# Pooling mixer of a two-layer diffusion step: padded input written by the producer, edge columns scaled apart, residual updates between the window groups

## The reference

```python
def pool_mixer(h, w, scale):
    for j, win in enumerate((2, 4, 8, 16)):
        xg = hf[..., j * 256:(j + 1) * 256]
        lo = jnp.clip(t - win // 2, 0, s)
        hi = jnp.clip(t + win // 2, 0, s)
        mean = (cs[:, hi] - cs[:, lo]) / (hi - lo)      # cs: running sum over tokens
        outs.append((mean - xg) @ w[j])
    return jnp.concatenate(outs, axis=-1) * scale
...
x = x + g1 * pool_mixer(modulate(x, norm_mix_g, sh1, sc1), ...)
h = modulate(x, norm_ffn_g, sh2, sc2)
x = x + g2 * peer(h, ...)
```

## Time and profile before

| | us |
|---|---|
| median of 3 runs | 3579.02 (3578.78 to 3579.57) |
| the profiled execution | 3577.18 |
| its span, first to last instruction | 3575.4 |
| TensorE busy | 3155.2 (88%) |
| VectorE busy | 3021.8 (85%) |
| ScalarE busy | 1053.4 (29%) |
| GpSimd busy | 1889.5 (53%) |

### The profile page before, as it was taken

How to read it: one execution, slowest core, us unless ns; L and a number is a source line. 1 busy time by engine, 2 the same in 40 slices (tenths; PEclk the granted TensorE clock), 3 DMA queues, 4 the chain that set the end, 5 groups by cost and what they waited for, 6 DMA issues and landing times.

```text
span 3575.4 us, 49897 instructions
## 1 busy us (share of the span) xinstructions
PE 3155.2 (88%) x15686; PEld 2598.6 (73%) x15686; DVE 3021.8 (85%) x5339; ACT 1053.4 (29%) x1587; POOL 1889.5 (53%) x1412
## 2 busy tenths in 40 slices
PE   6988999378999999999998496088999999999997
PEld 3554555167899999999997254077899999999996
DVE  1645279887999999999998679896999999999998
ACT  2122111043333333333333210044333333333332
POOL 0000012276677887777774012276677777767663
PEclk8999999689999999999999798589999999999999
DMA  4122144036999999999997010036999999999995
GB/s 195 47 94 74 71 174 166 14 159 255 408 409 406 399 403 387 401 404 405 400 396 299 25 48 0 0 164 270 407 410 408 403 404 393 409 409 400 404 405 214
DMA packets 244633, 995.72 MB, mean 278 GB/s; under 512 B 22608, under 2 KB 72528, under 8 KB 204880
## 3 DMA queue, kind: packets, MB, share of 16 engines
q0 software_dynamic: 147456, 536.94, 37.9%
q1 hardware_dynamic: 97104, 457.81, 32.5%
HBM read 941.44 MB, written 53.22 MB: 278 GB/s over the span
## 4 chain that ended last, share of the span: by engine, by line
PE 58%; DVE 23%; issue 9%; DMA 6%; POOL 2%; ACT 1%; DVEq 0%; POOLq 0%; SPq 0%; ACTq 0%
PE bankA L1094 7%; PE bankA L1092 7%; PE bankA L1093 7%; PE bankD L1080 6%; PE bankD L1105 5%; PE bankD L1106 5%; PE bankD L1104 5%; PE bankA L1177 3%; DMA rows<-in_v,idxc 3%; DVE acc L953 3%; PE bankA L1106 2%; PE bankA L1105 2%; PE bankA L1104 2%; PE bankD L1223 2%; DMA rows<-in_u,idxc 1%
## 5 line engine op out<-in xcount | busy, mean ns | idle before, releaser
L492 POOL DMA_INDIRECT rows<-in_u,idxc x512 | 748.6, 1462 | 233.7 <-issue 133.0
L492 POOL DMA_INDIRECT rows<-in_v,idxc x512 | 679.0, 1326 | 256.3 <-issue 134.3
L1092 PE MATMUL bankA<-hh,uh 128*128 128x384 f32 x2048 | 690.5, 337 | 22.7 <-ACT htok L562 13.8
L1094 PE MATMUL bankA<-hh,ul 128*128 128x384 f32 x2048 | 690.1, 337 | 0.0
L1093 PE MATMUL bankA<-hl,uh 128*128 128x384 f32 x2048 | 688.5, 336 | 0.0
L953 DVE SCALAR_TENSOR_TENSOR acc<-rows,a,acc 128x1024 f32<-128x1024 f32 x512 | 635.4, 1280 | 13.8 <-DMA rows<-in_v,idxc 12.5
L944 DVE CUSTOM_DVE_ANT_0 rows<-rows,htok 128x1024 f32<-128x1024 f32 x512 | 607.3, 1220 | 21.0 <-DMA rows<-in_u,idxc 19.2
L454 POOL TENSOR_TENSOR mask<-mask,topf 128x1280 f32<-128x1280 f32 x32 | 91.8, 2890 | 969.2 <-DVE mask L874 969.2
L546 ACT ACTIVATE wt<-bankA 128x384 f32<-128x384 f32 x256 | 125.9, 492 | 995.6 <-PE bankA L1094 756.4
L1177 PE MATMUL bankA<-hT,wch 128*128 128x512 f32 (+1 forms) x1344 | 385.7, 447 | 35.5 <-ACT hT L607 21.8
L1092 PEld LDWEIGHTS bankA<-hh,uh 128*128 128x128 f32 x2048 | 386.8, 189 | 35.1 <-ACT htok L562 14.4
(11 more groups left out here) (166 smaller groups left out, 4579.7 us busy)
## 6 DMA issues: line engine op xcount, KB each, us to landing
uraw<-in_uT SPq DMA_DIRECT2D x128, 1024.0 KB
vraw<-in_vP SPq DMA_DIRECT2D x128, 1024.0 KB
gates_scratch<-gbuf SPq DMA_DIRECT2D x12, 4096.0 KB, 11.6
gp<-gates_scratch SPq DMA_DIRECT2D x64, 768.0 KB
sq<-in_ada SPq DMA_DIRECT2D x14, 2048.0 KB, 7.9
wch<-in_ada SPq DMA_DIRECT2D x10, 2048.0 KB, 8.1
wch<-in_wq SPq DMA_DIRECT2D x8, 2048.0 KB, 8.1
rows<-in_u,idxc POOLq DMA_INDIRECT x512
```

The costliest lines, as they stand in the source:

```text
L492: pool.indirect_dma_start(out=rows[:, j, :], out_offset=None, in_=table.rearrange("l e d -> (l e) d"), in_offset=bass.IndirectOffsetOnAxis ...
L1092: pe.matmul(abank[c], hi, hh[:, k, :], start=k == 0, stop=False)
L1094: last = pe.matmul(abank[c], lo, hh[:, k, :], start=False, stop=k == K - 1)
```

## The change

- ScalarE's shift of `norm(2)` (and only of it) writes into `pads`, a padded buffer for all eight chunks, in place of `hT`. The padding columns are zeroed by three GpSimd memsets after the last `ob` unit; the memset of `pad` and the eight copies from `hT` into `pad` are gone.
- A group waits for its own two chunks, not for all eight.
- The window sums go from `pads` into `win2` and back and forth inside it, as before, with the same shapes.
- The table `inv` and its load are gone. The win - 1 edge columns of a segment are multiplied in place by win / count, from 26 new columns behind the constants (2 short instructions for window 2, 4 for the others), and one scalar_tensor_tensor for each segment does (sum * 1/win) - h, where a tensor_tensor with `inv` and a tensor_tensor subtraction stood.
- The residual updates of a group's two pool units stand behind the next group's work, in place of all eight behind the last group.

```diff
 C_ID, C_ONE, C_ROT, C_IO, C_SEL = 0, P, 2 * P, 3 * P, 4 * P
-N_CONST = 4 * P + 2
+C_RT = 4 * P + 2
+N_RT = sum(w - 1 for w in WINDOWS)
+N_CONST = C_RT + N_RT
...
-                inv = sb("inv", [P, 4, T], where=pl)
-                pad = sb("pad", [P, 3, 2, PW], where=pl)
+                pads = sb("pads", [P, K, PW], where=pl)
+                win2 = sb("win2", [P, 2, 2, PW], where=pl)
...
-                        sp.dma_start(inv[:, :, :], inv_d).then_inc(inv_ready, 16)
...
+                if L == 1:
+                    pool.wait_ge(d_full, Dn[("ob", 0, K - 1)] + 1)
+                    pool.memset(pads[:, :, 0:PAD], 0.0)
+                    pool.memset(pads[:, :, PAD + TS:3 * PAD + TS], 0.0)
+                    pool.memset(pads[:, :, PW - PAD:PW], 0.0).then_inc(pads_zeroed, 1)
...
+                            dst = [pads[:, k, q0:q1] if i == 2 else hT[:, k, a:b] for (a, b), (q0, q1) in zip(SEGS, PSEG)]
                             for c, (a, b) in enumerate(SEGS):
-                                last = act.activation(hT[:, k, a:b], hT[:, k, a:b], ACT.Identity,
+                                last = act.activation(dst[c], hT[:, k, a:b], ACT.Identity,
...
             def pooling():
-                v.wait_ge(inv_ready, 16)
-                v.wait_ge(h_ready, 3 * K)
-                then(v.memset(pad[:, :, :, :], 0.0))
+                v.wait_ge(pads_zeroed, 1)
+                edge = C_RT
                 for j, win in enumerate(WINDOWS):
-                    h2 = hT[:, 2 * j:2 * j + 2, :]
-                    for c, (a, b) in enumerate(SEGS):
-                        last = v.tensor_copy(pad[:, 0, :, PSEG[c][0]:PSEG[c][1]], h2[:, :, a:b])
-                    then(last)
-
-                    s, w, src = 1, PW, 0
+                    half = win // 2
+                    v.wait_ge(h_ready, 2 * K + 2 * j + 2)
+                    if j:
+                        v.wait_ge(pooled_ready, j)
+                    centre = pads[:, 2 * j:2 * j + 2, :]
+                    s, w, d, cur = 1, PW, 0, centre
                     while s < win:
                         w -= s
-                        dst = 1 if src != 1 else 2
-                        then(v.tensor_tensor(pad[:, dst, :, 0:w], pad[:, src, :, 0:w], pad[:, src, :, s:s + w], ALU.add))
-                        s, src = 2 * s, dst
+                        then(v.tensor_tensor(win2[:, d, :, 0:w], cur[:, :, 0:w], cur[:, :, s:s + w], ALU.add))
+                        s, d, cur = 2 * s, 1 - d, win2[:, d, :, :]
+                    for a, b in PSEG:
+                        sides = [(a - half, half, edge)]
+                        if half > 1:
+                            sides.append((b - win + 1, half - 1, edge + half))
+                        for p0, n, c in sides:
+                            last = v.tensor_tensor(cur[:, :, p0:p0 + n], cur[:, :, p0:p0 + n],
+                                                   const[:, c:c + n].unsqueeze(1).to_broadcast([P, 2, n]), ALU.mult)
+                    then(last)
+                    edge += win - 1
                     for c, (a, b) in enumerate(SEGS):
-                        p0 = PSEG[c][0] - win // 2
-                        last = v.tensor_tensor(sq[:, 2 * j:2 * j + 2, a:b], pad[:, src, :, p0:p0 + b - a],
-                                               inv[:, j, a:b].unsqueeze(1).to_broadcast([P, 2, b - a]), ALU.mult)
-                    then(last)
-                    v.tensor_tensor(sq[:, 2 * j:2 * j + 2, :], sq[:, 2 * j:2 * j + 2, :], h2, ALU.subtract
-                                    ).then_inc(pooled_ready, 1)
-                for m in range(K):
+                        q0, q1 = PSEG[c]
+                        last = v.scalar_tensor_tensor(out=sq[:, 2 * j:2 * j + 2, a:b], in0=cur[:, :, q0 - half:q1 - half],
+                                                      scalar=1.0 / win, in1=centre[:, :, q0:q1],
+                                                      op0=ALU.mult, op1=ALU.subtract)
+                    last.then_inc(pooled_ready, 1)
+                    if j:
+                        for m in (2 * j - 2, 2 * j - 1):
+                            update(("pool", m), m, (1, 2))
+                for m in (K - 2, K - 1):
                     update(("pool", m), m, (1, 2))
```

More of the change, by code:

```diff
@@ L128, in build @@
 def build(nc, ins, outs):
-    xT_d, small_d, const_d, trig_d, inv_d, ck_d, cv_d, ada_d, qkv_d, wo_d, pw_d, wq_d, keys_d, u_d, v_d, uT_d, vP_d = ins
+    xT_d, small_d, const_d, trig_d, ck_d, cv_d, ada_d, qkv_d, wo_d, pw_d, wq_d, keys_d, u_d, v_d, uT_d, vP_d = ins
     y_d, nk_d, nv_d = outs
@@ L257, in build @@
         keys_ready = sem("keys_ready")
-        inv_ready = sem("inv_ready")
+        pads_zeroed = sem("pads_zeroed")
         chunk_ready = [sem(f"chunk_ready{i}") for i in range(2)]
@@ L1267, in shape_constants @@
     trig = np.stack([np.cos(ang), np.sin(ang)], 1).astype(np.float32)
[L1268 to L1274, removed]
+    edges = []
+    for w in WINDOWS:
+        h = w // 2
+        counts = [t + h for t in range(h)] + [m + h for m in range(h - 1, 0, -1)]
+        edges += [np.float32(w) * (np.float32(1.0) / np.float32(n)) for n in counts]
+    const[:, C_RT:C_RT + N_RT] = np.array(edges, np.float32)
+    return const, trig
 def kernel(x_prompt, x_sample, cache_k, cache_v, c, c_ctx, ada_w, ada_b, norm_mix_g, norm_ffn_g,
@@ L1293 @@
         + [arr["attn_q_norm_g"].T, arr["attn_k_norm_g"].T, cols(arr["pool_scale"])], 1)
-    const, trig, inv = shape_constants()
+    const, trig = shape_constants()
     ck = np.ascontiguousarray(arr["cache_k"][0, 0].transpose(2, 1, 0))
@@ L1306 @@
                               ).reshape(DEPTH, PAIRS, P, 2 * D)
-    ins = dict(xT=xT, small=small, const=const, trig=trig, inv=inv, ck=ck, cv=cv, ada=ada, qkv=qkv, wo=wo, pw=pw,
+    ins = dict(xT=xT, small=small, const=const, trig=trig, ck=ck, cv=cv, ada=ada, qkv=qkv, wo=wo, pw=pw,
                wq=wq, keys=keys, u=arr["peer_u"], v=arr["peer_v"], uT=uT, vP=vP)
```

## The result

| | before | changed |
|---|---|---|
| median, same chip | 3579.3 (3575.53 to 3584.36, 6 runs) | 3557.17 (3554.52 to 3566.86, 6 runs) |
| the profiled execution | 3577.18 | 3554.52 |
| its span | 3575.4 | 3552.7 |

The ratio is 0.9942, with a 95% interval of 0.993 to 0.9954: 16 to 25 us. The forecast was 3560.6, from 3557.0 to 3567.0.

The account below looks back on a forecast made before the run. The prediction took an unbroken chain without DMA, mostly VectorE's pooling work and then TensorE's units, as the bound. Group 3 ending 8.5 us earlier and fewer units behind it gave 18.4 us off 3579.02: 3560.6, range 3557 to 3567.

Parts of the forecast that it names:

- the signs at its end: Changed profile: pair 1.6 to 1.7 us, norm(3)'s root 42 to 45 after the scaling, dense stages as before, clock recovering.
- The start: VectorE before group 0: last-shift wait, 0.92 us issue and memset go; first sum at about 1973.14; about 6.4 us gained.
- A group: VectorE's work per group: sums 1.59 us each, copies of 0.93 gone, product and subtraction replaced, edges 1.6 in all.
- The fused pair: VectorE's two scalar_tensor_tensor instructions per group, replacing product and subtraction: 1.68 us, lower bound 1.56.
- The walk: VectorE's groups 0 to 3 timed in turn: group 3 ends at 2001.7, not 2010.24, 8.5 us earlier.
- The sum of parts: Split of the 8.5 us: start 6.4, copies 3.7, product and subtraction 5.6, less edges 1.6 and updates some 6.
- Behind group 3: Unit 6 starts 0.98 us later; two TensorE units, not six, take 4.32 or 6.44, then norm(3)'s sum 8.67.
- The clock: TensorE at unit 6, half or full clock uncalled: gain 18.4 us, between 17.4 and 19.5.
- Rival 1: TensorE's clock stays low through units 6 and 7, gain 15.2, or norm(3)'s sum too, 6.5; chance 0.12 with Rival 4.
- Rival 2: Gain lost later, in layer 1's routing or experts waiting for something that doesn't move: 3579 us; chance 0.03.
- Rival 3: Buffers starting 96 bytes later slow the dense expert stage: 3586 us at 0.1 us a step; chance 0.04 as slower.
- Rival 4: Dearer edge products, 0.9 us, or updates waiting for TensorE at half clock, 2.2 more: 3564; chance 0.12 with Rival 1.

Follow-up runs that it names:

- e5_wait_all: The changed kernel, but every group waits for all eight chunks of ScalarE's shift: 3559.58 us (one run), stretch 43.1 against 41.6.
- e7_copies: The changed kernel, but ScalarE writes hT as before and VectorE copies each group into the padded buffer: 3558.84 us (one run), stretch 45.5.
- e6_edges2: The changed kernel with every edge product done a second time, by a factor of 1: 3555.1 us (one run), stretch 43.3.
- e8_pointer: The changed kernel with the fused instruction's factor 1/win read from a column in SBUF, not a number in the instruction: 3556.39 us (one run), stretch 41.9.
- e10_after: The changed kernel again, unchanged, in another batch: 3557.21 us, ratio 0.9938 to the kernel before, stretch 44.4.
- e12_after: The changed kernel a third time, unchanged: 3554.12 us, ratio 0.9945 to the kernel before, stretch 44.0.
- e4_after256: The changed kernel with 64 new columns of constants in place of 26, so later buffers start 256 bytes later: 3556.86 us, ratio 0.9944, stretch 41.6.
- e1_shift: The kernel before with only 26 unused columns behind the constants, so later buffers start 96 bytes later: 3576.11 us, ratio 0.9997, stretch 62.1.
- e9_gpsimd: The changed kernel with the first window sum of each group on GpSimd: 3561.07 us, ratio 0.9951 to the kernel before.

## Why the prediction was right

**The number.** 3557.17 lies 3.4 us under the forecast and 0.2 over the lower bound, and by the medians the gain is 22.1 us: the prediction gave 0.01 to more than 21. That this median stands inside the range is partly luck. The mechanism stands on the rows: 20.5 us in the stretch of the first profile, 17.7 and 18.1 in two others, where the sum had 19.5 with full clock and 17.4 with half. Of the signs at its end, the dense stages lasted as before (layer 1's within 0.3 us, layer 0's within 1.8) and the clock came back. Two missed: the pair took 1.56 us and not 1.6 to 1.7, and norm(3)'s root came at 41.6 in the first profile, ahead of 42 to 45.

**The start.** Forecast within 0.1 us behind the scaling; it came 0.1 before its end. e5_wait_all and e7_copies give the old wait and the copies back at their price.

**A group.** The window sums, 1.59 start to start, held (1972.95 to 1974.54). The edges: forecast 1.6 us, measured 0.26 + 0.42 + 0.42 + 0.46 = 1.6 (starts in e6_edges2 and the changed kernel). The fused pair was mis-sized: 1.68 forecast, 1.56 measured, its lower bound. The rows that I took it from read the factor from SBUF, and e8_pointer shows that this is the 0.12.

**The walk.** Group 3 was to end 28.6 us behind the scaling, and ended 27.3 behind it: 0.5 from the pairs, 0.1 at the start, and 0.6 because an update starts before the pair ahead of it has drained, and a sum before the update has (from a pair's end to the next sum it took 1.9 and 1.8 us where I had 2.2 and 2.0). The wait for unit 1 was there at the size forecast, 0.16 against 0.1. In e10_after and e12_after, where it was 1.2 and 1.0, group 3 ended 28.5 and 28.2 behind. The sum of parts that followed the walk was wrong, though the walk wasn't: it counted the copies of group 0 twice, at the start and among the 3.7, and took "some 6" us for the updates where only four stand ahead of group 3's end, 3.8 us (1980.02 - 1978.02 and 1988.51 - 1986.67). By the measured pieces: 5.6 (start) + 3.7 (copies) + 5.9 (product and subtraction less pair) - 1.6 (edges) - 3.8 (updates) = 9.8, which is 37.1 - 27.3.

**Behind group 3.** 0.97 to unit 6 and 8.67 for the sum are as forecast; the two units at full clock took 4.59 where I had 4.32. Together 14.3 us in place of 25.0.

**The clock.** The prediction wouldn't call it and took the middle of 17.4 and 19.5. Four executions of the changed kernel (with e4_after256) gave 20.5, 20.5, 17.7 and 18.1, two of each kind; their mean is 19.2, not 18.4, by the cheaper pair and the shorter walk. The pause of 4.1 us before unit 6 took units 4 and 5 at 6.44 us, as units 0 and 1 had been before. They took 7.24 in the first profile, so the pause was 2.84, and 6.16 and 6.03 in e10_after and e12_after, where it was 3.93 and 4.06. By page "TensorE: Matmul & The Clock Gate" of the Trainium skill, section on HAM oscillation, a kernel whose bursts are parted by waits starts each of them at half clock. Behind the pauses of 3.93 and 4.06 us it was so, behind those of 2.84 it wasn't, and e7_copies kept the full clock over 3.65. Rival 1, a clock that stays low through units 6 and 7 and the sum, was seen in none.

**The rivals.** Rival 2: most of the gain arrived at the end. From norm(3)'s root to the program's last root it took 1525.8 us before and 1526.1 in e1_shift, and 1526.6 to 1527.4 in the four profiles of the changed kernel (with e4_after256), so about 1 us was lost later; layer 1's dense stage kept its 1069 us. Rival 3 was tested alone and isn't seen: the dense stage stays within 0.5 us in e1_shift and e4_after256. Rival 4's dear edges and long waits came to 0 and, at most, 1.2 us for unit 1.

**What stays open.** The four ratios to the kernel before, 0.9942, 0.9944, 0.9938 and 0.9945, mean 0.58% or 20.7 us, where the stretches average 19.2. Each interval is wider than that difference. The work behind the stretch doesn't fill it, as it gives about 1 us back: most of this is TensorE's first `wq` piece, 20.3 us after 19.4, whose granted clock rose 5.5 us after its start where it rose 3.7 after before. Whether the load of `inv`, which is gone, has a share was not tested.

## What to carry to other kernels

Find the work by the chain, not by the busy shares: 11 us less work, 2 us less waiting for it and a change of order were worth 20.5, and the order's part (5.2 us alone, 7.5 beside the rest at full clock) takes nothing away from any engine. When a consumer holds a double-buffered bank, look at where its release stands in the consumer's program: six units waited for eight small updates behind the last group. Prices from rows held to a few hundredths of a microsecond where the instruction's form was the same to the operand (sums, copies, edges); the pair's was 8% off, since where the factor comes from is part of the form. And an idle engine is no free engine: GpSimd's four sums cost VectorE 8.7 us for 6.4 saved.

## What the runs showed of the hardware that I had not expected

- A scalar_tensor_tensor pair of 1024 and 256 elements takes 1.56 us with its factor in the instruction and 1.68 with the factor in a column of SBUF; the first is the price of a tensor_tensor pair of these shapes.
- Four dependent-free products of 2 to 16 columns take 0.38 to 0.43 us in a row, 0.08 each behind the first, where one alone lasts 0.15 to 0.18.
- Beside each GpSimd sum of 2.6 to 2.7 us one VectorE instruction with two SBUF inputs stood until the sum was done: 2.51 us for a scaling of 128x128 that takes 0.35 (e9_gpsimd).
- The same program differs by 2.4 to 2.8 us in one stretch of 42, mostly by whether TensorE's clock falls near its last burst; in one profile it fell about 1.0 us after a burst had begun, behind a pause of 2.76.
